# Seven-product pairs of a gated FFN: the next pair's first product ahead of this pair's last, a third buffer, low parts moved between two engines

## The chip, the cores and the metric

The kernel runs on one core of a Trainium2 chip (trn2). The metric is the device time of one execution in microseconds (us); lower is better. Five engines work side by side, each through its own queue and in order: TensorE (PE, matmuls; PEld is its weight load), VectorE (DVE), ScalarE (ACT), GpSimd (POOL) and SyncE (SP), which here issues the transfers. Engines wait for each other through counting semaphores.

## The reference, cut to what matters

Two layers of a decoder run over 512 prompt tokens and 64 new tokens (TOK = 576 columns), with model width 1024. A layer is FFN, token mixer, FFN, so that four FFNs take part:

```python
def ffn_half(h, g_pre, g_post, w_in, w_out):
    a = rmsnorm(h, g_pre) @ w_in
    gate, up = jnp.split(a, 2, axis=-1)
    return h + FFN_RESID * rmsnorm((jax.nn.silu(gate) * up) @ w_out, g_post)
```

`w_in` is 1024 x 5632 and `w_out` 2816 x 1024, all float32. The diff touches only how `rmsnorm(h) @ w_in` and the gate after it are computed and scheduled.

## The kernel before, in words

**Precision.** A float32 operand is split into a high part (ACT copies it to the fp32r type, `x_hi`, `w_hi`) and a low part (the rest, a subtraction, `x_lo`, `w_lo`). A product is three fp32r matmuls: high x high, high x low, low x high.

**Stages.** Six stages follow each other: ffn, mla, ffn, ffn, gla, ffn. In an FFN the input product has two phases. The first, "classic" phase takes 8 blocks of weights (128 x 1024, one block is one gate or up tile) straight: slots `raw[i]`, `w_hi[i]`, `w_lo[i]`, four of each. ACT makes the high part (line 754), POOL the low part (line 1233).

**The pairs.** The second phase takes the other 36 blocks as 18 pairs (`GRP` = 18), a gate block and an up block each. A pair's 2 x 2 block product is done in seven half-size products instead of eight (a Strassen-Winograd form): the weight blocks a11, a12, a21, a22 (128 x 512) give the sums s1 = a21 + a22, s2 = s1 + a11, s3 = a11 + a21, s4 = s2 + a12 (DVE, line 1563), and the activations give b11, b21, b22 and four sums t_0 to t_3 (each 128 x 4 x 288). PE computes in this order; `f_p` counts the products:

| product | weights x activations | PSUM bank | waits for |
|---|---|---|---|
| P1 | a11 x b11 | A, fresh | low part of a11 (POOL) |
| P2 | s1 x t_0 | C, fresh | low part of s1 (DVE) |
| P3 | s2 x t_3 | A, added | low part of s2, copy of P1 made |
| P4 | s4 x b22 | C, added | low part of s4, copy of P2 made |
| P5 | s3 x t_1 | A, added | low part of s3, copy of P3's state made |
| P6 | a12 x b21 | B, fresh | low part of a12 (POOL) |
| P7 | a22 x t_2, plain float32 | A, added | DVE has read A after P5 |

P1 to P6 are 12 matmuls each at line 2313, 128 x 288; P7 is 8 instructions at line 2353. Banks A, B, C alternate between two sets from pair to pair.

**DVE in pair g** (`group`, line 1643 on): last half of pair g-1 (line 1615, reads bank A after P7 of g-1), low part of s4 (line 1590), low part of the gated result of g-1 (line 1495), low part of s3, then s1 of pair g+1, P4's bank plus a copy (line 1597), scaling (1602), s2 of g+1, bank A after P5 (1636), product of the two (1640), low part of s1 of g+1, s4 of g+1, P6's bank plus the copy (1597), scaling (1602), s3 of g+1, low part of the gated result (1495 and 1497), low part of s2 of g+1. **ACT in pair g**: silu of g-1 (line 900), high part of s3 (873), high part of the gated result of g-1 (904, waits for DVE's line 1615), copy of P1's bank (896), copies after P2 and P3, high parts of a11 and s1 of g+1, silu, high parts of s2, s4, a12 of g+1. **POOL** does the low parts of a11 and a12 (line 1250). **SP** loads the four parts of pair g+1 (line 627): a22 into one of two buffers, the other three after all four sums of pair g stand.

**Ahead of the pairs.** DVE rebuilds x from its halves (`whole`, four times 128 x 1152, line 1540) and forms t_0 to t_3 (lines 1551, 1556) between the classic blocks, with POOL making the low parts of blocks 4 to 7 meanwhile.

Of the kernel before, what the change touches and what calls it, by code (L numbers as in the profile page):

```python
# [7 lines left out]
F32 = mybir.dt.float32  # L8
# [64 lines left out]
def hybrid_step(nc, io, stages=STAGES):  # L73
    pre_gain = PRE_GAIN
    with ExitStack() as ctx:
# [67 lines left out]
        t_f = [sb(f"t_f{i}", [P, HK, HALF], offset=h_at + i * T_W) for i in range(4)]  # L143
        t_lo = {i: sb(f"t_lo{i}", [P, HK, HALF], F32R, offset=h_at + i * T_W) for i in (0, 1, 3)}
# [183 lines left out]
        def forms(st):  # L328
# [13 lines left out]
            return made[r]  # L342

# [240 lines left out]
        def _(sp):  # L584
# [25 lines left out]
            def ffn(st):  # L610
# [15 lines left out]
                def part(dst, row_of, c, landed, g, i):  # L626
                    sp.dma_start(dst[:, :], w_in[f, FB + 2 * g + row_of + 4 * i, :, c * HK * P:(c + 1) * HK * P]).then_inc(landed, 16)

                def four(g, i):

                    a = g0 + g
                    if g >= 2:
                        sp.wait_ge(f_p, 7 * (a - 1) + 14 * i)
                    part(w[f"a22_{g % 2}"], 1, 1, f_a2[g % 2], g, i)
                    sp.wait_ge(f_sum, 4 * (a - 1) + 3 + 8 * i)
                    sp.wait_ge(f_alo, 2 * a + 4 * i)
                    part(w["a12"], 0, 1, f_a12, g, i)
                    sp.wait_ge(f_sum, 4 * a + 8 * i)
                    part(w["a21"], 1, 0, f_a2[g % 2], g, i)
                    part(w["a11"], 0, 0, f_a11, g, i)  # L640
# [109 lines left out]
        def _(act):  # L750
# [94 lines left out]
            def ffn(st):  # L845
# [56 lines left out]
                def high_part(g, c, n, half, i):
                    act.wait_ge(f_gu, n + 4 * i)
                    act.activation(gu[:, CLASSIC + g + 2 * i, half * HALF:(half + 1) * HALF], c[:, :], ACT.Copy).then_inc(s_guhi, 1)

                def last_half(g, i):
                    gate(c_1[g % 2], 5 * (g0 + g) + 5, i)

                def group(g, i, more):
# [1982 lines left out]
```

## Time and profile before

| | us |
|---|---|
| median of 3 runs | 2428.88 (2423.8 to 2429.35) |
| the profiled execution's own time | 2426.47 |
| its span on the core | 2424.8 |

| engine | busy us | share of the span |
|---|---|---|
| PE | 2308.0 | 95% |
| PEld | 2039.3 | 84% |
| DVE | 1336.3 | 55% |
| ACT | 967.8 | 40% |
| POOL | 685.5 | 28% |

The page says that a busy PE is not a PE at its peak, since matmuls overlap in the pipeline; so the start times of consecutive matmuls are what tells a wait. A row of the timeline gives the start in us from the span's start, the duration in us, engine, line, operation, tiles and shapes, and in square brackets the idle time of that engine just before it with what ended it.

### The profile page before, as it was taken

To read this page: it belongs to the slowest core of one execution; us is meant where nothing else is said; L and a number is where in the kernel's file an instruction comes from. 1 tells how busy PE (TensorE), PEld (TensorE's weight loads), DVE (VectorE), ACT (ScalarE), POOL (GpSimd) and SP (SyncE) were. 2 spreads that over 40 slices of the span, in tenths; PEclk is the share of its full clock that TensorE was granted. 3 is DMA by queue.
4 is the path that set the end of the run, shared out by engine and by line. 5 is a ranking of instruction groups with operands and counts; after the bars stand their busy time and mean duration, and the time that the engine had idled before them with its cause. 6 is when DMAs were issued, how large, how long until landed. Compare 5 with 4: busy or idle time off the path is not lost.

```text
span 2424.8 us, 37992 instructions
## 1 busy us (share of the span) xinstructions
PE 2308.0 (95%) x14176; PEld 2039.3 (84%) x14176; DVE 1336.3 (55%) x2545; ACT 967.8 (40%) x2014; POOL 685.5 (28%) x441
## 2 busy tenths in 40 slices
PE   8899999999899999999999999999999999999998
PEld 7888988986456889998888898888999789899887
DVE  5888700586421588881058888104566647788401
ACT  5445412614221645552254455225322444455322
POOL 2222243240312322224332222432344222222332
PEclk9999999999998999999999999999999999999999
DMA  3222332232671322224232222422211332222422
GB/s 124 74 88 83 97 122 87 70 111 82 196 233 53 109 79 87 83 75 144 87 109 79 87 88 71 145 86 82 70 53 56 152 99 98 75 87 84 143 85 84
DMA packets 100292, 237.53 MB, mean 98 GB/s; under 512 B 12268, under 2 KB 29165, under 8 KB 99854
## 3 DMA queue, kind: packets, MB, share of 16 engines
q1 hardware_dynamic: 97038, 224.62, 28.7%
q0 software_dynamic: 3072, 10.49, 1.3%
q8 instruction: 114, 1.87, 0.3%
q14 instruction: 68, 0.56, 0.1%
HBM read 220.17 MB, written 14.89 MB: 97 GB/s over the span
## 4 chain that ended last, share of the span: by engine, by line
PE 70%; DVE 8%; issue 8%; ACT 4%; SPq 3%; POOL 2%; DMA 2%; DVEq 0%; ACTq 0%; POOLq 0%
PE psum L2313 24%; PE psum L2251 7%; PE psum L2252 7%; PE psum L2253 7%; PE psum L2353 5%; PE psum L2117 3%; PE psum L2119 3%; PE psum L2118 3%; POOL w_lo L1233 2%; PE psum L2245 2%; PE psum L2244 2%; DVE s_r L1563 1%; SPq L493 1%; PE psum L2675 1%; ACT c L896 1%
## 5 line engine op out<-in xcount | busy, mean ns | idle before, releaser
L1233 POOL TENSOR_TENSOR w_lo<-raw,w_hi 128x1024 fp32r<-128x1024 f32 (+1 forms) x173 | 416.8, 2416 | 813.6 <-ACT w_hi L754 813.2
L1250 POOL TENSOR_TENSOR a_lo_r<-a_r,a_hi_r 128x512 fp32r<-128x512 f32 x144 | 193.0, 1341 | 700.6 <-ACT a_hi_r L873 485.7
L754 ACT ACTIVATE w_hi<-raw 128x1024 fp32r<-128x1024 f32 (+1 forms) x179 | 187.2, 1048 | 478.8 <-DMA raw<-ffn_out 349.7
L1394 DVE TENSOR_TENSOR y<-psum,g_post 128x512 f32<-128x512 f32 x48 | 32.5, 689 | 548.8 <-ACT y L768 548.2
L2117 PE MATMUL psum<-x_hi,w_hi 128*128 128x256 f32 (+1 forms) x1008 | 304.7, 302 | 0.3
L2118 PE MATMUL psum<-x_lo,w_hi 128*128 128x256 f32 (+1 forms) x1008 | 299.7, 297 | 0.0
L2119 PE MATMUL psum<-x_hi,w_lo 128*128 128x256 f32 (+1 forms) x1008 | 299.7, 297 | 0.0
L2251 PE MATMUL psum<-w_hi,gu 128*128 128x512 f32 x704 | 275.8, 392 | 0.6
L2252 PE MATMUL psum<-w_hi,gu 128*128 128x512 f32 x704 | 274.0, 389 | 0.0
L2253 PE MATMUL psum<-w_lo,gu 128*128 128x512 f32 x704 | 274.0, 389 | 0.0
L2313 PE MATMUL psum<-t_lo,s_hi_r 128*128 128x288 f32 x864 | 254.5, 295 | 0.0
L2313 PE MATMUL psum<-t_hi,s_hi_r 128*128 128x288 f32 x576 | 175.1, 304 | 49.0 <-ACT c L896 41.4
L873 ACT ACTIVATE s_hi_r<-s_r 128x512 fp32r<-128x512 f32 x288 | 181.1, 629 | 74.9 <-DVE s_r L1563 74.9
L1590 DVE TENSOR_TENSOR s_lo_r<-s_r,s_hi_r 128x512 fp32r<-128x512 f32 x288 | 199.4, 694 | 0.0
L2117 PEld LDWEIGHTS psum<-x_hi,w_hi 128*128 128x128 f32 x1008 | 192.9, 191 | 4.3 <-issue 1.8
L2118 PEld LDWEIGHTS psum<-x_lo,w_hi 128*128 128x128 f32 x1008 | 193.1, 192 | 0.2
L2119 PEld LDWEIGHTS psum<-x_hi,w_lo 128*128 128x128 f32 x1008 | 192.8, 191 | 0.0
L2313 PE MATMUL psum<-x_hi,a_hi_r 128*128 128x288 f32 x576 | 184.9, 321 | 3.5 <-DVE work L1483 3.5
L2313 PE MATMUL psum<-x_hi,s_lo_r 128*128 128x288 f32 x576 | 170.3, 296 | 0.0
L2313 PE MATMUL psum<-x_hi,s_hi_r 128*128 128x288 f32 x576 | 170.1, 295 | 0.0
L2313 PE MATMUL psum<-x_lo,a_hi_r 128*128 128x288 f32 x576 | 169.7, 295 | 0.0
L2313 PE MATMUL psum<-x_hi,a_lo_r 128*128 128x288 f32 x576 | 169.6, 294 | 0.0
(318 smaller groups left out, 5101.8 us busy)
## 6 DMA issues: line engine op xcount, KB each, us to landing
a_r<-ffn_in SPq DMA_DIRECT2D x288, 256.0 KB, 3.2
raw<-ffn_out SPq DMA_DIRECT2D x88, 512.0 KB, 3.5
raw<-ffn_in SPq DMA_DIRECT2D x32, 512.0 KB, 3.6
raw<-gla_in SPq DMA_DIRECT2D x25, 512.0 KB, 3.5
cache<-cache POOLq DMA_DIRECT2D x64, 160.0 KB, 4.9
cache<-cache SPq DMA_DIRECT2D x64, 160.0 KB, 5.1
c_k<-cache_kt SPq DMA_DIRECT2D x64, 128.0 KB, 3.1
keep<-h SPq DMA_DIRECT2D x12, 512.0 KB, 6.3
```

The lines of the kernel that those rows point to most:

```text
L754: act.activation(w_hi[slot][:, 0:w], raw[slot][:, 0:w], ACT.Copy).then_inc(s_hi, 1)
L873: act.activation(dst[:, :], src[:, :], ACT.Copy).then_inc(f_hi, 1)
L1233: pool.tensor_tensor(w_lo[slot][:, 0:w], raw[slot][:, 0:w], w_hi[slot][:, 0:w].bitcast(F32), ALU.subtract).then_inc(s_lo, 1)
L1250: pool.tensor_tensor(w[f"{name}_lo"][:, :], w[name][:, :], w[f"{name}_hi"][:, :].bitcast(F32), ALU.subtract).then_inc(f_alo, 1)
L1590: dve.tensor_tensor(w[f"{name}_lo"][:, :], w[name][:, :], w[f"{name}_hi"][:, :].bitcast(F32), ALU.subtract).then_inc(f_lo, 1)
L2117: pe.matmul(out, wh, xh, start=start, stop=False)
L2118: pe.matmul(out, wh, xl, start=False, stop=False)
L2119: return pe.matmul(out, wl, xh, start=False, stop=stop)
L2251: pe.matmul(dst, w[0], m[0], start=start, stop=False)
L2252: pe.matmul(dst, w[1], m[0], start=False, stop=False)
L2253: return pe.matmul(dst, w[0], m[1], start=False, stop=stop)
L2313: last = pe.matmul(out[:, 0:HALF], y, m[:, k, :], start=fresh and first, stop=end, skip_group_check=not fresh)
```

## The change

**PE.** P1 of pair g+1 is issued between P6 and P7 of pair g (`first`). Its bank condition is the single eviction or the last half of pair g-1.

**Buffers.** a22 has three buffers, by g mod 3: the two of before, and columns 288 to 415 of the first four k-rows of `x_lo`, which no product of the pairs reads. Rows there are 512 bytes with a stride of 2304 bytes. SP then loads a21 as soon as s3 of the pair before stands, a22 once P7 of three pairs back is done, a11 after POOL's low part of the last a11, and a12 after s4 and a12's low part.

**DVE and ACT order.** In pair g DVE now does: last half of g-1, low of s3, low of the gated result of g-1, s1 and s2 of g+1, P4's bank, scaling, bank A after P5, s3 and s4 of g+1, the product, P6's bank, scaling, low of s1, low of the gated result, low of s2, low of s4 (all g+1). ACT does: high of g-1's result, high of a11, copy after P2, high of s1, copy after P3, high of s2, silu, high of s3, high of s4, high of the result, silu of the second half, high of a12, copy of P1 of g+1. POOL keeps the low parts of a11 and a12.

**Ahead of the pairs.** The four `whole` go to the end of the stage before (`pre_factors`), into tiles `x_f` in space of `gu` not yet used; the low parts of classic blocks 4 to 7 go from POOL to DVE (`w_low`). All counts on semaphores follow.

```diff
+        x_f = [sb(f"x_f{i}", [P, HK, HALF], offset=g_at + (CLASSIC + i) * 2 * W4) for i in range(4)]
+        a22_x = sb("a22_x", [P, HK, TOK], offset=x_at + DT * W4)
...
+        def a_22(st, g):
+
+            if g % 3 == 2:
+                return a22_x[:, :, HALF:HALF + P]
+            return forms(st)[f"a22_{g % 3}"][:, :].rearrange("p (k c) -> p k c", k=HK)
... SP
+                for g in range(1, GRP):
+                    a = g0 + g
+                    sp.wait_ge(f_sum, 4 * (a - 1) + 3)
+                    part(w["a21"][:, :], 1, 0, f_a2[g % 2], g)
+                    if g == 2:
+                        sp.wait_ge(f_x, 8 * (f + 1))
+                    if g >= 3:
+                        sp.wait_ge(f_p, 7 * (a - 2) + 1)
+                    part(a_22(st, g), 1, 1, f_a2[g % 2], g)
+                    sp.wait_ge(f_alo, 2 * (a - 1) + 1)
+                    part(w["a11"][:, :], 0, 0, f_a11, g)
+                    sp.wait_ge(f_sum, 4 * a)
+                    sp.wait_ge(f_alo, 2 * a)
+                    part(w["a12"][:, :], 0, 1, f_a12, g)
... ACT
+                def copy_first(g):
                     a = g0 + g
+                    act.wait_ge(s_gulo, c0 + (2 * a if g == 0 else 2 * (a - 1)))
+                    copy_out(c_1[g % 2], ring(st, g, 0), first_product(g, a))
+
+                def group(g):
+                    a, more = g0 + g, g < GRP - 1
                     if g > 0:
...
+                        high_part(g - 1, c_1[(g - 1) % 2], 2 * a, 0)
                     if g == 0:
                         act.wait_ge(s_unit, u0 + 4 * CLASSIC)
-                        x_form(1, 6)
+                        x_form(1, 7)
+                    if more:
+                        hi_a11(a + 1)
...
+                    copy_out(c_3, ring(st, g, 1), 7 * a + 2)
+                    if more:
+                        hi_sum("s1", a + 1, 1, 2)
...
+                    copy_out(c_2, ring(st, g, 0), 7 * a + 3)
                     if more:
...
+                        hi_sum("s2", a + 1, 2, 3)
...
+                    gate(c_2, 5 * a + 2)
                     if more:
...
+                        hi_sum("s3", a + 1, 3, 5)
+                        hi_sum("s4", a + 1, 4, 4)
+                    high_part(g, c_2, 2 * a + 1, 1)
+                    gate(c_1[g % 2], 5 * a + 5)
                     if more:
...
+                        hi_a12(a + 1)
+                        copy_first(g + 1)
... POOL
             def ffn(st):
-                n = first_block[st] + SLOTS
-                pool.wait_ge(s_lo, n)
-                for j in range(FB - SLOTS):
-                    low(n + j)
...
+                for a in range(g0, g0 + GRP):
+                    part_low("a11", a, 1, 1)
+                    part_low("a12", a, 6, 6)
+                pool.wait_ge(s_lo, first_block[st] + FB)
... DVE
             def pre_factors(b):
 
+                if stages[b] == "ffn":
+                    for i in (0, 1, 3):
+                        whole(b, i)
                 dve.wait_ge(s_hroot, 2 * b + 2)
...
+                w_low(b0 + 4)
                 for hf in range(2):
                     gate_low(q0 + hf, hf, 0)
+                w_low(b0 + 5)
...
+                def group(g):
+                    a, more = g0 + g, g < GRP - 1
                     if g > 0:
...
+                        last_half(g - 1)
+                    low_form("s3", g, 4, 3)
                     if g > 0:
...
+                        low_part(g - 1, c_1[(g - 1) % 2], 2 * a, 0)
+                    if more:
+                        sum_1(g + 1)
                     if g == 0:
                         x_low_form(1, 3)
                     if more:
...
+                        sum_2(g + 1)
+                    plus(c_2, ring(st, g, 1), 3 * a + 3, 7 * a + 4)
+                    scaled(c_2, 1, 5 * a + 1)
...
+                    if more:
+                        sum_3(g + 1)
+                        sum_4(g + 1)
...
+                    plus(c_1[g % 2], ring(st, g, 2), 3 * a + 1, 7 * a + 6)
+                    scaled(c_1[g % 2], 0, 5 * a + 4)
                     if more:
...
+                        low_form("s1", g + 1, 2, 2)
+                    low_part(g, c_2, 2 * a + 1, 1)
                     if more:
...
+                        low_form("s2", g + 1, 3, 4)
+                        low_form("s4", g + 1, 5, 4)
... PE
+                def first(g):
+                    a = g0 + g
+                    pe.wait_ge(f_alo, 2 * a + 1)
+                    if g < 2:
+                        pe.wait_ge(s_evicted, u0 + 4 * CLASSIC - RING + 3 * g + 1)
+                    else:
+                        pe.wait_ge(f_gu, 2 * (a - 1))
+                    product(ring(st, g, 0), "a11", b_11, True)
...
                     product(b_b, "a12", b_21, True)
...
+                    if g < GRP - 1:
+                        first(g + 1)
+                    pe.wait_ge(f_c, 5 * a + 3)
```

## Rows read from the trace of the kernel before

**Rows 1.** Windows, one per FFN's pairs: length, busy us of each engine, clock, DMA.

```profile
73.73:299.20 225.47, 211.02 (x1441) 199.57 (x1441) 181.45 (x326) 112.13 (x236) 49.27 (x36) 1.00 0.27 87
875.23:1099.40 224.17, 211.03 (x1441) 199.58 (x1441) 180.02 (x326) 111.93 (x236) 49.72 (x36) 1.00 0.28 88
1298.88:1523.20 224.32, 211.08 (x1441) 199.63 (x1441) 180.09 (x326) 111.95 (x236) 49.71 (x36) 1.00 0.28 88
2050.40:2278.20 227.80, 213.63 (x1441) 201.66 (x1441) 180.38 (x326) 112.09 (x236) 49.24 (x36) 0.99 0.27 86
```

**Rows 2.** Timeline of PE in one settled pair: first matmul of each product.

```profile
939.79 0.51 PE L2313 MATMUL psum<-x_hi,a_hi_r 128*128 128x288 f32 x1
...
941.59 0.30 PE L2313 MATMUL psum<-t_hi,s_hi_r 128*128 128x288 f32 x1
...
943.88 0.37 PE L2313 MATMUL psum<-t_hi,s_hi_r 128*128 128x288 f32 x1 [0.54 <-ACT c L896]
...
945.55 0.29 PE L2313 MATMUL psum<-x_hi,s_hi_r 128*128 128x288 f32 x1
...
950.32 2.10 PE L2353 MATMUL psum<-t_f,a_r 128*128 128x288 f32 x8
952.05 0.51 PE L2313 MATMUL psum<-x_hi,a_hi_r 128*128 128x288 f32 x1
```

**Rows 3.** Timeline of DVE in the same pair.

```profile
940.37 1.49 DVE L1495 TENSOR_TENSOR gu<-c,gu 128x224 fp32r<-128x224 f32 x1
...
941.91 0.68 DVE L1590 TENSOR_TENSOR s_lo_r<-s_r,s_hi_r 128x512 fp32r<-128x512 f32 x1
942.51 0.44 DVE L1615 SCALAR_TENSOR_TENSOR c<-psum,c 128x288 f32<-128x288 f32 x1
942.88 0.68 DVE L1590 TENSOR_TENSOR s_lo_r<-s_r,s_hi_r 128x512 fp32r<-128x512 f32 x1
...
947.42 0.46 DVE L1597 TENSOR_TENSOR c<-psum,c 128x288 f32<-128x288 f32 x1 [1.37 <-PE psum L2313]
947.91 0.51 DVE L1602 TENSOR_TENSOR c<-c,r_pre 128x288 f32<-128x288 f32 x1
```

**Rows 4.** Timeline of DVE at the last pair's end: line 1495 alone.

```profile
1099.06 0.38 DVE L1495 TENSOR_TENSOR gu<-c,gu 128x224 fp32r<-128x224 f32 x1
```

**Rows 5.** Timelines of ACT and POOL in the same settled pair.

```profile
942.99 0.45 ACT L904 ACTIVATE gu<-c 128x288 fp32r<-128x288 f32 x1 [1.88 <-DVE c L1615]
943.34 0.69 ACT L896 ACTIVATE c<-psum 128x288 f32<-128x288 f32 x2
...
946.12 0.62 ACT L873 ACTIVATE a_hi_r<-a_r 128x512 fp32r<-128x512 f32 x1
...
940.25 1.36 POOL L1250 TENSOR_TENSOR a_lo_r<-a_r,a_hi_r 128x512 fp32r<-128x512 f32 x1 [4.31 <-PE psum L2353]
946.82 1.29 POOL L1250 TENSOR_TENSOR a_lo_r<-a_r,a_hi_r 128x512 fp32r<-128x512 f32 x1 [5.21 <-ACT a_hi_r L873]
```

**Rows 6.** Timelines of the first pair (second FFN): PE, DVE, SP, ACT.

```profile
875.23 0.40 PE L2313 MATMUL psum<-x_hi,a_hi_r 128*128 128x288 f32 x1 [0.87 <-DVE work L1483]
...
877.71 0.69 DVE L1563 TENSOR_TENSOR s_r<-s_r,a_r 128x512 f32<-128x512 f32 x1
...
881.42 1.28 SPq L627 DMA_DIRECT2D a_r<-ffn_in  x3
...
886.02 0.63 ACT L873 ACTIVATE a_hi_r<-a_r 128x512 fp32r<-128x512 f32 x1 [3.14 <-DMA a_r<-ffn_in]
```

**Rows 7.** Timelines ahead of the pairs (second FFN): DVE, and PE at block 7.

```profile
833.64 0.18 DVE L1432 RECIPROCAL h_r<-h_r 128x4 f32<-128x4 f32 x1 [3.51 <-ACT h_r L804]
...
863.16 1.35 DVE L1551 TENSOR_TENSOR t_f<-t_f,t_f 128x1152 f32<-128x1152 f32 x1
...
867.80 0.28 PE L2117 MATMUL psum<-x_hi,w_hi 128*128 128x256 f32 x1
```

**Rows 8.** Timeline of PE, first pair of the last FFN: P7.

```profile
2065.93 0.85 PE L2353 MATMUL psum<-t_f,a_r 128*128 128x288 f32 x1 [3.60 <-DVE c L1636]
```

More of the change, by code:

```diff
@@ L624, in ffn, with part @@
                 w, g0 = forms(st), GRP * f
[L626 to L640, printed above, removed]
+                def part(dst, row_of, c, landed, g):
+                    src = w_in[f, FB + 2 * g + row_of, :, c * HK * P:(c + 1) * HK * P]
+                    sp.dma_start(dst, src.rearrange("p (k c) -> p k c", k=HK) if len(dst.shape) == 3 else src).then_inc(landed, 16)
@@ L642, in ffn @@
                 classic_out(sp, st, 0)
                 wait_keep(sp, st)
-                part(w["a21"], 1, 0, f_a2[0], 0, 0)
-                part(w["a22_0"], 1, 1, f_a2[0], 0, 0)
-                part(w["a11"], 0, 0, f_a11, 0, 0)
+                part(w["a21"][:, :], 1, 0, f_a2[0], 0)
+                part(a_22(st, 0), 1, 1, f_a2[0], 0)
+                part(w["a11"][:, :], 0, 0, f_a11, 0)
                 classic_out(sp, st, 2)
-                part(w["a12"], 0, 1, f_a12, 0, 0)
+                part(w["a12"][:, :], 0, 1, f_a12, 0)
@@ L900, in gate, with high_part @@
                     act.activation(c[:, :], c[:, :], ACT.Silu).then_inc(s_silu, 1)
[L902 to L909, printed above, removed]
+                def high_part(g, c, n, half):
+                    act.wait_ge(f_gu, n)
+                    act.activation(gu[:, CLASSIC + g, half * HALF:(half + 1) * HALF], c[:, :], ACT.Copy).then_inc(s_guhi, 1)
@@ L1587, in low_form, with sum_3, sum_4 @@
+                def sum_3(g):
+                    add("s3", w["a11"], w["a21"], g0 + g, 5)
+                def sum_4(g):
+                    a = g0 + g
+                    dve.wait_ge(f_sum, 4 * a + 2)
+                    dve.wait_ge(f_a12, 16 * (a + 1))
+                    add("s4", w["s2"], w["a12"], a, 4)
+                def low_form(name, g, hi, summed):
                     a = g0 + g
-                    dve.wait_ge(f_hi, 6 * a + hi + 12 * i)
-                    dve.wait_ge(f_sum, 4 * a + summed + 8 * i)
+                    dve.wait_ge(f_hi, 6 * a + hi)
+                    dve.wait_ge(f_sum, 4 * a + summed)
@@ L2358, in ffn @@
                 pair(3)
-                group(0, 0)
-                group(1, 0)
-                for i in range((GRP - 2) // 2):
-                    group(2, i)
-                    group(3, i)
+                first(0)
+                for g in range(GRP):
+                    group(g)
                 pe.wait_ge(s_gulo, 2 * FT * f + 2 * CLASSIC)
```

273 lines of the change are left out of this document (106 added, 167 removed).

## The prediction

> **What bounds the kernel now.** I read the table of busy shares first: PE is busy 95% of the span, DVE 55%, so DVE's average hides nothing by itself. Then the windows, one for each FFN's 18 pairs [rows 1]: they are 225.47, 224.17, 224.32 and 227.80 us long, 901.76 us in all, 37% of the span, and PE is idle 13.1 to 14.5 us in each. Then PE's timeline of one settled pair [rows 2]. It lasts 952.05 - 939.79 = 12.26 us. Six products of 12 matmuls take 1.59 us each where nothing waits (950.32 - 945.55 = 4.77 for P4 to P6), P7 takes 1.73, and the product behind P7 takes 1.80. So a pair without a wait would take 1.80 + 5 x 1.59 + 1.73 = 11.48 us. The missing 0.78 us is one hole: P2 starts at 941.59, P3 at 943.88, 0.70 more than 1.59 (the row's idle 0.54 starts from the modelled end), and P3 itself, restarted, takes 0.08 more (943.88 to 945.55). It is ended by ACT's copy of P1's bank.
>
> Why is that copy late? Backwards [rows 3, 5]: the copy starts at 943.34, behind ACT's line 904 (942.99), which waits for DVE's line 1615 (942.51), which is queued behind line 1590 (941.91) and line 1495 (940.37). That last one took 1.49 us, where the same instruction alone takes 0.38 [rows 4]: 1.11 us more, and POOL's low part of a11 runs from 940.25 to 941.61 beside it. An instruction of DVE with two SBUF inputs that comes 0.12 us after POOL's waits until POOL is through.
>
> The Trainium skill ("SBUF — State Buffer", Who interferes with whom) says that the second of two such instructions blocks for the whole of the first; here 1.11 us of POOL's 1.29 to 1.36 are lost, and the measurement decides.
>
> **The change part by part.**
>
> *P1 ahead of P7.* Its copy now has P7 and P2 (1.73 + 1.80 us) before P3 wants it, instead of P2 alone. The 0.78 us hole goes, if nothing takes its place. Three things could be late next; I walk one pair with the start of P2 as 0, so P3 starts at 1.80, P4 3.39, P5 4.98, P6 6.57, P1 of the next pair 8.16, P7 9.75, P2 again 11.48. A product's bank can be read 1.87 us after its start (P4 at 945.55, DVE's line 1597 at 947.42) [rows 2, 3]. Steps on DVE: 0.60 for a 512-wide instruction (941.91 to 942.51), 0.37 for a 288-wide one (942.51 to 942.88), 0.49 from the addition to the scaling that needs it; lines 1495 and 1497 together 941.91 - 940.37 - 1.11 = 0.43 [rows 3, 4]. ACT: 0.35 from line 904 to the next, 0.52 for a 512-wide high part (0.62 less the 0.10 overlap seen at 942.99), 0.48 from DVE's line 1615 to ACT's 904, 0.54 from a copy's start to PE's product [rows 2, 3, 5].
>
> DVE is free until P5's bank can be read: 4.98 + 1.87 = 6.85. From there its queue is full: bank A 0.37, s3 0.60, s4 0.60, product 0.37, addition 0.49, scaling 0.37, low of s1 0.60, low of the result 0.43, low of s2 0.60, then POOL's low part of a12, whose high part ACT finishes in just this stretch, 1.11, then low of s4 0.60. That is 6.14, up to 12.99. The last half follows and frees ACT 0.48 later (13.47), ACT writes the high part of the result (0.35), the high part of a11 (0.52), and the copy after P2, which lets P4 of the next pair start 0.54 later: 14.88. P4 is due at 11.48 + 3.39 = 14.87. So a second loop, P4 to P4 over DVE, POOL and ACT, takes 1.59 + 1.87 + 6.14 + 0.48 + 0.35 + 0.52 + 0.54 = 11.49 us, against PE's own 11.48. The two are equal; since any scatter of one then adds, I take 11.55.
>
> *Without that cover* the other waits have room. The low part of s1 starts at 9.65 and is there at 10.4 for P2 at 11.48; that of s2 at 11.4, or 12.5 behind the lock, for P3 at 13.28; the copy after P3 lets P5 go at about 4.7, due at 4.98. The transfers: SP is released by s3 (starts at 7.22, stands at 7.9) instead of by all four sums; the third of three loads is used 3.75 us after its issue (882.27, when the first starts at 881.42, to 886.02) [rows 6], so a11 is there at 7.9 + 0.9 + 3.75 = 12.6, 1.2 us before ACT wants it at 13.8. The strided third buffer (512-byte pieces, which this row does not show) may take some tenths more or nothing: bounds 0 and 1 us, both inside the 1.2.
>
> *The first pair.* P1 of pair 0 no longer waits for both evictions (idle 0.87 [rows 6]), but P3 does not profit. DVE begins s3 at 877.71 as before, s4 stands at 879.05, ACT's high parts of s4 and a12 take 2 x 0.52, the copy starts at 880.1, P3 at 880.6. Then ACT's order puts the high part of a11 ahead of the copy after P2, and a11 lands only at 878.5 + 0.85 + 3.75 = 883.1; P4 starts at 883.1 + 0.52 + 0.54 = 884.2 where 882.2 was due: a new stall of 1.9 us, between 0 (load in time) and 3. P2 of pair 1 then starts 4 x 1.59 + 1.73 later, at 892.2, which is 17.0 us after the window's start.
>
> *Ahead of the pairs.* The first three `whole` at 1.27 us each (1.35 less overlap, a like 128 x 1152 instruction at 863.16) fill DVE's idle 3.51 us ahead of the reciprocals [rows 7]: 0.3 us too long, with ACT and PE still on other work, so 0. The low parts of four classic blocks go to DVE at about 1.2 us each. The tightest is block 7: DVE is at 863.16, two sums of 1.27 and the low part 1.2 make 866.9, PE wants it at 867.80 [rows 7]. So 0, from -0.2 to 1 us per FFN if that cover goes. POOL's idle time costs nothing. Its locks on DVE vanish there, which frees nothing on PE.
>
> **The sum.** An FFN's window is 17.0 (to P2 of pair 1) + 16 T + 9.9 (pair 17: 1.80 + 4 x 1.59 + 1.73). With T = 11.55 it is 211.7, four of them 846.8, against 901.8: 55 us less. On the profiled execution's own time, 2426.5, this gives 2371.5; the median of the runs is 2.4 us higher, so 2374.
>
> **The rivals.** 0.1 us in T is 6.4 us.
>
> *A, better:* the DVE loop does not bind and a11 lands in time: T 11.48 and the front's 1.9 us gone, 4.5 + 7.6 less: 2362. For it: the loops are equal only to 0.01. Against it: ACT's order.
>
> *B, half way:* POOL's low part of a11 gets in ahead of s1 in part of the pairs. In the walk the order of the two is close: after line 1615 DVE starts s1 1.35 us later (0.48 + 0.45 + 0.05 for ACT's result, 0.37 for its low part), POOL arrives 0.48 + 0.35 + 0.62 + 0.08 = 1.53 later (0.08 as from 946.74 to 946.82 [rows 5]). If DVE loses, s1 is 1.1 us later, its high part too, and the copy after P3 behind it, so P5 stalls. The loop is then 1.87 + 6.14 + 0.48 + 0.35 + 0.70 + 1.11 + 0.73 + 0.52 + 0.54 = 12.44. In the six pairs of each FFN with the strided buffer (s1 waits for it): 4 x 6 x 0.9 = 21 us: 2396.
>
> *C, no change:* the same in all pairs: T = 12.44, 17 + 199 + 9.9 = 226, 904 in all: 2431. The 0.18 us margin speaks against it.
>
> *D, slower:* as C, and each of POOL's two locks costs its whole 1.29 instead of 1.11 (the arrival falls at the start of a DVE instruction, and both loops carry both): T = 12.8, 4 x (26.9 + 204.8) = 926.8: 2454. It is slower by over 0.3% from T = 12.5 on. Against it: row 940.37.
>
> *E:* on the forecast's loop the lock costs the whole of POOL's 1.36 instead of 1.11: T = 11.74 and 2386. Row 940.37 speaks against it too.
>
> The Trainium skill ("SBUF — State Buffer", Who interferes with whom) states the rule behind E, the second waits for the whole of the first; this case's row shows 1.11 us.
>
> *F:* the two stalls of the first pair let the clock drop, as in the last FFN, where after 3.60 idle the first instruction of P7 took 0.85 [rows 8] and P7 4.2 instead of 2.1 us. 3 us per FFN, 12 in all: 2386.
>
> *G, it does not do what it says:* P1 of the next pair finds its bank taken. It needs the last half of pair g-1, done at about 2.0, and is due at 8.16. I give this nothing.
>
> **How the numbers follow.** Forecast 0.60, A 0.10, B 0.12, C 0.05, D 0.06, E and F together 0.07. The forecast's own spread is T from 11.48 to 11.7, 2369 to 2384. The range reaches over A, E, F and to B: 2360 to 2397. It leaves out C, D and a part of B. 0.3% is 7 us, about what a measurement of this kernel can tell: faster 0.89 (forecast, A, B, E, F), within 0.3% 0.05 (C), slower 0.06 (D).
>
> **What would show each step.** PE's timeline: line 2313 on a11 directly ahead of line 2353, pairs 11.5 to 11.6 apart, no idle time ahead of P3. Windows of 210 to 213 us. Ahead of P4 at most 0.1 us idle, ended by ACT's line for the copy. DVE: a low part (line 1590's successor) of about 1.8 us once per pair, the one of s4. First pair: about 2 us ahead of P4, with ACT waiting for a11's transfer. Wrong would be: idle time ahead of P5 (B, C), a11's landing later than 5 us in settled pairs, or PE waiting at block 7 for a low part.

## The result, and the profile after

| | before | after |
|---|---|---|
| median of the runs, us | 2427.38 (4 runs) | 2366.01 (4 runs, 2361.64 to 2368.19) |
| profiled execution's own time, us | 2426.47 | 2368.19 |
| its span, us | 2424.8 | 2366.5 |
| PE busy, share of the span | 95% | 97% |

The ratio is 0.9747, 95% interval 0.9726 to 0.9767: 61 us or 2.5% faster; 2374 was forecast, 55 less than the 2428.88 known then. It was measured again beside the experiments: 2363.41 (5 runs), ratio 0.9743 (0.9727 to 0.9759).

The windows of the four FFNs' pairs in the changed kernel, as in [rows 1] (window, its length, busy us of PE, PEld, DVE, ACT and POOL, clock, DMA share, GB/s):

```profile
72.77:283.80 211.03, 208.37 (x1442) 199.64 (x1441) 190.71 (x321) 110.08 (x233) 60.75 (x36) 1.00 0.29 93
861.05:1072.72 211.67, 208.49 (x1442) 199.62 (x1441) 190.66 (x321) 110.11 (x233) 60.05 (x36) 1.00 0.29 93
1271.27:1482.43 211.16, 208.38 (x1442) 199.63 (x1441) 190.83 (x322) 110.14 (x233) 60.67 (x36) 1.00 0.30 93
2008.78:2219.85 211.07, 208.36 (x1442) 199.62 (x1441) 190.69 (x322) 110.11 (x233) 60.69 (x36) 1.00 0.30 93
```

Together they are 844.9 us, against 901.8 before: 56.8 of the 58.3 us that the profiled executions differ by. PE is now idle 2.7 to 3.2 us in a window instead of 13.1 to 14.5. From the second pair on, the time from P2 to P2 is 11.58 us in the mean instead of 12.33, over 64 pairs 48 us less. The first pairs give 6 us, nearly all of it in the last FFN (14.5 us instead of 20.2), where P7 had waited 3.60 us before [rows 8] and the granted clock was 0.66 from 2062.30 to 2070.20. DVE and POOL are each busy some 10 us more per window: they block each other more than before, in places where it mostly costs nothing.

One settled pair (one that follows another pair of its FFN) of the second FFN. PE: P7 of the pair before, then P2, P4 and P7 of this one, as [rows 2]:

```profile
933.47 2.10 PE L2362 MATMUL psum<-t_f,a_x 128*128 128x288 f32 x8
935.20 0.51 PE L2313 MATMUL psum<-t_hi,s_hi_r 128*128 128x288 f32 x1
938.61 0.37 PE L2313 MATMUL psum<-x_hi,s_hi_r 128*128 128x288 f32 x1
945.04 2.10 PE L2362 MATMUL psum<-t_f,a_r 128*128 128x288 f32 x8
```

P7 to P7 is 945.04 - 933.47 = 11.57 us, against 12.26. The starts of all seven products, read off the same timeline with P2 as 0, are P3 1.81, P4 3.41, P5 5.09, P6 6.68, P1 of the next pair 8.26, P7 9.84. The hole ahead of P3 is gone; the one product that is too long is P4, 1.68 us instead of 1.59. Of the 64 pairs that follow another settled pair, 63 lie within 0.03 of 11.57. The other one takes 11.93: there a11 lands late and P4 waits 0.20 us for the copy behind it.

```profile
1053.58 0.63 ACT L883 ACTIVATE a_hi_r<-a_r 128x512 fp32r<-128x512 f32 x1 [0.24 <-DMA a_r<-ffn_in]
```

(P7's operand `a_x` is the third buffer; P7 itself shows no difference.)

DVE in that pair, as [rows 3]:

```profile
934.43 2.37 DVE L1596 TENSOR_TENSOR s_lo_r<-s_r,s_hi_r 128x512 fp32r<-128x512 f32 x2
936.72 0.45 DVE L1621 SCALAR_TENSOR_TENSOR c<-psum,c 128x288 f32<-128x288 f32 x1
...
938.06 0.68 DVE L1569 TENSOR_TENSOR s_r<-a_r,a_r 128x512 f32<-128x512 f32 x1
938.91 1.53 DVE L1569 TENSOR_TENSOR s_r<-s_r,a_r 128x512 f32<-128x512 f32 x1 [0.16 <-PE psum L2313]
...
942.16 0.46 DVE L1641 SCALAR_TENSOR_TENSOR c<-psum,c 128x288 f32<-128x288 f32 x1 [0.65 <-PE psum L2313]
...
946.00 2.38 DVE L1596 TENSOR_TENSOR s_lo_r<-s_r,s_hi_r 128x512 fp32r<-128x512 f32 x2
948.30 0.44 DVE L1621 SCALAR_TENSOR_TENSOR c<-psum,c 128x288 f32<-128x288 f32 x1
```

ACT and POOL, as [rows 5]:

```profile
937.20 0.45 ACT L914 ACTIVATE gu<-c 128x288 fp32r<-128x288 f32 x1 [2.44 <-DVE c L1621]
937.55 0.62 ACT L883 ACTIVATE a_hi_r<-a_r 128x512 fp32r<-128x512 f32 x1
938.08 0.39 ACT L906 ACTIVATE c<-psum 128x288 f32<-128x288 f32 x1
```

```profile
934.54 1.71 POOL L1253 TENSOR_TENSOR a_lo_r<-a_r,a_hi_r 128x512 fp32r<-128x512 f32 x1 [6.22 <-ACT a_hi_r L883]
938.25 1.64 POOL L1253 TENSOR_TENSOR a_lo_r<-a_r,a_hi_r 128x512 fp32r<-128x512 f32 x1 [2.00 <-ACT a_hi_r L883]
```

This is the forecast's second loop, from P4 to P4 over DVE, POOL and ACT. From bank A's reading to the last half DVE's queue is never empty: 948.30 - 942.16 = 6.14 us, with POOL's 1.71 us beside the low part of s4 (two such instructions take 2.38 instead of 1.29). Then ACT: 0.48 to line 914, 0.88 to the copy, 0.53 to P4.

The first pair (second FFN), as [rows 6]: PE, then DVE's sums and ACT.

```profile
865.73 0.37 PE L2313 MATMUL psum<-t_hi,s_hi_r 128*128 128x288 f32 x1 [1.35 <-DVE s_lo_r L1596]
869.20 0.37 PE L2313 MATMUL psum<-x_hi,s_hi_r 128*128 128x288 f32 x1 [1.64 <-ACT c L906]
```

```profile
862.81 0.69 DVE L1569 TENSOR_TENSOR s_r<-a_r,a_r 128x512 f32<-128x512 f32 x1
```

```profile
868.13 0.63 ACT L883 ACTIVATE a_hi_r<-a_r 128x512 fp32r<-128x512 f32 x1 [1.44 <-DMA a_r<-ffn_in]
868.66 0.39 ACT L906 ACTIVATE c<-psum 128x288 f32<-128x288 f32 x1
```

P4 waits 1.64 us for a copy that stands behind a11's landing: the stall that was forecast, at 1.9.

### The profile page after: what moved, and what is told of

Read it like the earlier page. It is cut to its first block, busy times and chain, and to the rows that moved or that the text cites. A ratio compares the mean times of both kernels' runs of the same rounds, so it can differ in the third digit from the quotient of the medians.

```text
span 2366.5 us, 38028 instructions
## 1 busy us (share of the span) xinstructions
PE 2297.0 (97%) x14176; PEld 2039.4 (86%) x14176; DVE 1372.5 (58%) x2561; ACT 964.2 (41%) x2014; POOL 688.8 (29%) x425
## 3 DMA queue, kind: packets, MB, share of 16 engines
q8 instruction: 114, 1.87, 0.3%
## 4 chain that ended last, share of the span: by engine, by line
PE 85%; DVE 5%; SPq 3%; ACT 3%; DMA 2%; issue 2%; POOL 0%; DVEq 0%; ACTq 0%; POOLq 0%
PE psum L2313 28%; PE psum L2251 7%; PE psum L2252 7%; PE psum L2253 7%; PE psum L2117 6%; PE psum L2362 6%; PE psum L2119 6%; PE psum L2118 6%; PE psum L2244 2%; PE psum L2245 2%; SPq L501 1%; PE psum L2682 1%; DMA a_r<-ffn_in 1%; ACT y L778 1%; SPq L552 1%
## 5 line engine op out<-in xcount | busy, mean ns | idle before, releaser
L1240 POOL TENSOR_TENSOR w_lo<-raw,w_hi 128x1024 fp32r<-128x1024 f32 (+1 forms) x157 | 373.6, 2386 | 743.4 <-ACT w_hi L764 743.2
L1253 POOL TENSOR_TENSOR a_lo_r<-a_r,a_hi_r 128x512 fp32r<-128x512 f32 x144 | 239.7, 1665 | 708.8 <-ACT a_hi_r L883 708.8
L1596 DVE TENSOR_TENSOR s_lo_r<-s_r,s_hi_r 128x512 fp32r<-128x512 f32 x288 | 268.9, 955 | 0.8
L2313 PE MATMUL psum<-t_hi,s_hi_r 128*128 128x288 f32 x576 | 185.0, 321 | 5.4 <-DVE s_lo_r L1596 5.4
L2313 PE MATMUL psum<-x_hi,s_hi_r 128*128 128x288 f32 x576 | 175.4, 304 | 5.9 <-ACT c L906 5.9
L2313 PE MATMUL psum<-x_hi,a_hi_r 128*128 128x288 f32 x576 | 169.4, 294 | 0.0
```

What stands on the lines that cost most here:

```text
L1240: pool.tensor_tensor(w_lo[slot][:, 0:w], raw[slot][:, 0:w], w_hi[slot][:, 0:w].bitcast(F32), ALU.subtract).then_inc(s_lo, 1)
L1253: pool.tensor_tensor(w[f"{name}_lo"][:, :], w[name][:, :], w[f"{name}_hi"][:, :].bitcast(F32), ALU.subtract).then_inc(f_alo, 1)
L1596: dve.tensor_tensor(w[f"{name}_lo"][:, :], w[name][:, :], w[f"{name}_hi"][:, :].bitcast(F32), ALU.subtract).then_inc(f_lo, 1)
L2313: last = pe.matmul(out[:, 0:HALF], y, m[:, k, :], start=fresh and first, stop=end, skip_group_check=not fresh)
```

## Experiments

Each kernel was run beside the kernel before, on the same chip; ratios are to that kernel. T is the median time from P2 to P2 of the settled pairs, "first pair" the same time for pair 0 (the median of the four FFNs, or the spread), both in us in the profiled execution.

| kernel | median us (runs) | ratio (95%) | T | first pair |
|---|---|---|---|---|
| after, again | 2363.41 (5) | 0.9743 (0.9727 to 0.9759) | 11.57 | 14.5 |
| P1 behind P7 | 2363.7 (4) | 0.9747 (0.9728 to 0.9766) | 11.59 | 14.9 |
| swap alone | 2462.3 (4) | 1.0148 (1.0123 to 1.0172) | 12.8 | 14.5 to 17.5 |
| copy order alone | 2405.99 (4) | 0.9896 (0.9862 to 0.993) | 12.02 | 15.5 to 20.2 |
| copy ahead of a11 | 2353.6 (5) | 0.9707 (0.969 to 0.9725) | 11.49 | 13.4 |
| no low a12 | 2362.37 (4) | 0.9725 (0.9696 to 0.9755) | 11.53 | 14.6 |
| low s4 behind last half | 2385.16 (4) | 0.9813 (0.9777 to 0.9849) | 11.94 | 14.5 |
| low parts back | 2364.65 (4) | 0.9742 (0.971 to 0.9773) | 11.57 | 15.3 (one 17.4) |
| two a22 buffers | 2492.96 (6) | 1.0266 (1.0237 to 1.0295) | 13.4 | 14.5 |
| copy ahead of a11, again | 2354.68 (5) | 0.9701 (0.9679 to 0.9723) | 11.49 | 13.5 |
| + first copy early | 2352.97 (5) | 0.9694 (0.9668 to 0.972) | 11.49 | 13.5 |
| + both copies early | 2352.01 (5) | 0.9683 (0.9659 to 0.9707) | 11.49 | 13.2 (one 13.9) |

### P1 behind P7, in the changed kernel

```
                     product(b_b, "a12", b_21, True)
-                    if g < GRP - 1:
-                        first(g + 1)
...
                     last.then_inc(f_p, 1)
+                    if g < GRP - 1:
+                        first(g + 1)
```

> The changed kernel with one thing undone: PE issues P1 of the next pair behind P7 again, as before the change (counts on f_p follow). Theory Q (the queues did it): P1 starts 9.75 us into the pair, its bank can be read at 11.7, ACT has been free since 10.8 and copies at once, so P3, due at 13.3, never waits; the loop P4 to P4 over DVE, POOL and ACT is untouched. T stays 11.57, the time is 2366, within 3. Theory S (the step of the prediction: the swap itself removes the hole, since the copy needs P7 and P2 as cover): the 0.7 us ahead of P3 comes back, T about 12.25, 2366 + 64 x 0.68 = 2410.

Measured: 2363.7, single pairs 11.56 to 11.61, P3 1.59 us after P2 with no wait. Undoing the swap costs nothing that the times can tell. The hole is not closed by the place of P1.

### The swap alone, in the kernel before

```
+                    if g < GRP - 1:
+                        first(g + 1)
...
-                    product(b_a, "a11", b_11, True)
```

> The kernel before with the PE swap alone: P1 of the next pair ahead of P7, all queues of DVE, ACT, SP and POOL in their old order. Theory Q: the copy of P1 stands behind line 904 and line 1615 in their queues wherever P1 is; P7 is done before line 1615's turn in either order. T stays 12.26 and the hole stays ahead of P3: 2427, within 4. Theory S: T falls to about 11.5, 2427 - 64 x 0.7 = 2382 or less.

Measured: 2462.3, 36 us slower than before, which neither theory gave. The hole ahead of P3 grew. PE's group of P2 and P3 (line 2313), first in the kernel before, then in this one, and the wait in one pair of this one; columns of the groups: busy us, mean ns, idle before with its releasers.

```profile
L2313 PE MATMUL psum<-t_hi,s_hi_r 128*128 128x288 f32 x576 | 175.1, 304 | 49.0 <-ACT c L896 41.4 <-DVE s_lo_r L1590 7.6
```

```profile
L2313 PE MATMUL psum<-t_hi,s_hi_r 128*128 128x288 f32 x576 | 191.2, 332 | 81.4 <-ACT c L896 73.8 <-DVE s_lo_r L1590 7.6
```

```profile
996.91 0.38 PE L2313 MATMUL psum<-t_hi,s_hi_r 128*128 128x288 f32 x1 [1.32 <-ACT c L896]
```

```profile
995.55 0.45 DVE L1615 SCALAR_TENSOR_TENSOR c<-psum,c 128x288 f32<-128x288 f32 x1
...
999.48 0.69 DVE L1563 TENSOR_TENSOR s_r<-a_r,a_r 128x512 f32<-128x512 f32 x1 [1.92 <-DMA a_r<-ffn_in]
1000.45 0.46 DVE L1597 TENSOR_TENSOR c<-psum,c 128x288 f32<-128x288 f32 x1 [0.28 <-PE psum L2313]
1000.95 1.47 DVE L1602 TENSOR_TENSOR c<-c,r_pre 128x288 f32<-128x288 f32 x1
```

The wait on the copy, which stands behind line 1615, is 73.8 of the 81.4 us, against 41.4 of 49.0 before. P7, now a product later, frees a22's buffer later, and SP's loads for the pair stand behind that: DVE's s1 waits for its data until 2.57 us after P3 (999.48 - 996.91), in the kernel before until 1.47 after it (P3 at 943.88 [rows 2]):

```profile
945.35 0.69 DVE L1563 TENSOR_TENSOR s_r<-a_r,a_r 128x512 f32<-128x512 f32 x1 [0.82 <-DMA a_r<-ffn_in]
```

ACT's high part of a11 and POOL's low part come late with it, and POOL's lock, which fell into DVE's idle time, now falls on the scaling: 1.47 us where it took 0.51 [rows 3]. So P3 to P3 carries a second lock: 13.1 us in that pair. A part of the 36 us is the clock: in six places PE's matmuls start 0.24 us apart instead of 0.13 (83 of them, an estimate of 9 us), for example behind a wait of 2.07 us ahead of P3, with a granted clock of 0.58 from 906.70 to 910.50. The chain is read from the trace and not shown by a run of its own; the next experiment shows a lock that falls into the same stretch of DVE's queue, and the one with two buffers shows what it costs when the other loads stand behind a22's.

### The copy's place in ACT's queue alone, in the kernel before

```
-                    if g > 0:
-                        high_part(g - 1, c_1[(g - 1) % 2], 2 * a, 0, i)
...
                     copy_out(c_1[g % 2], ring(st, g, 0), a, 1, i)
+                    if g > 0:
+                        high_part(g - 1, c_1[(g - 1) % 2], 2 * a, 0, i)
```

> The kernel before with one edit: ACT takes the copy of P1's bank ahead of the high part of the gated result of the pair before (line 904) instead of behind it. PE's order, DVE's order, SP's order and the buffers are those of before. Theory Q (ACT's order made the hole; the place of P1 on PE is worth nothing): the copy runs when P1 is done, P3 starts 1.80 us after P2, T falls from 12.26 to 11.5 to 11.6, 68 pairs by 0.7 us is 48 less: 2380, between 2375 and 2390. Rival (the copy was only the last of several equal waits; low s2 on DVE or the copy after P2 takes its place at once): T stays above 12, 2410 or more.

Measured: 2405.99, 21 us less. PE's two groups that changed:

```profile
L2313 PE MATMUL psum<-t_hi,s_hi_r 128*128 128x288 f32 x576 | 176.1, 306 | 8.4 <-DVE s_lo_r L1590 8.0
L2353 PE MATMUL psum<-t_f,a_r 128*128 128x288 f32 x576 | 163.1, 428 | 13.1 <-DVE c L1636 12.1
```

Of the 41.4 us that P3 waited for ACT at most 0.4 are left; two moved lines did that. But T fell only from 12.25 (the same median in the kernel before) to 12.02, a third of the 0.7 us that I expected: DVE's queue, with both of POOL's locks in it, is late next. The first pairs also got longer (15.5 to 20.2 us, before 14.2 to 20.2), mostly by PE's wait for line 1636 ahead of P7, which is 12.1 us in all against 6.0 before.

```profile
978.69 0.46 DVE L1602 TENSOR_TENSOR c<-c,r_pre 128x288 f32<-128x288 f32 x1
979.07 1.78 DVE L1563 TENSOR_TENSOR s_r<-s_r,a_r 128x512 f32<-128x512 f32 x1
980.77 0.44 DVE L1636 SCALAR_TENSOR_TENSOR c<-psum,c 128x288 f32<-128x288 f32 x1
```

The lock falls on s2, directly ahead of the reading of bank A that P7 needs (P7 at 981.27). That is where the rival was right. What takes it away is the changed kernel's order on DVE, with s1 and s2 at the head of the pair and s3 and s4 behind bank A: there the same s2 takes 1.53 us (938.91) and the readings of P4's and P5's banks still come in time. How much of that is DVE's order and how much the earlier loads (here s1 still waits for its data until 977.60) no run shows apart.

### The copy after P2 ahead of the high part of a11

```
-                    if more:
-                        hi_a11(a + 1)
                     if a >= 1:
                         act.wait_ge(f_gu, 2 * a - 1)
                     copy_out(c_3, ring(st, g, 1), 7 * a + 2)
                     if more:
+                        hi_a11(a + 1)
```

> The changed kernel with two steps of ACT's queue swapped: the copy after P2 ahead of the high part of a11. Loop theory: the loop over DVE, POOL and ACT that ends at P4 loses 0.52 us and no longer binds, T falls from 11.57 to PE's own 11.48 (17 x 4 x 0.09 = 6 us), and the first pair's wait for a11's landing ahead of P4 (1.5 to 1.8 us in the trace) goes, 4 x 1.6 = 6: 12 us less than the changed kernel, about 2354. Rival: the 0.09 us is PE's own (the matmuls ahead of P5 are slower for another reason): 6 us less, about 2360. Second rival: POOL's low part of a11, now 0.35 later, falls on s2, and P5 or P6 waits: no gain or a loss.

Measured: 2353.6, and 2354.68 when it was measured again. P7 to P7 in the latter:

```profile
935.83 2.10 PE L2361 MATMUL psum<-t_f,a_r 128*128 128x288 f32 x8
947.32 2.10 PE L2361 MATMUL psum<-t_f,a_r 128*128 128x288 f32 x8
```

11.49 us, PE's own time, and the first pair is 1.1 us shorter. So the second loop did bind, as walked, with one term missing (below).

### GpSimd without its reading of a12

```
+                    if name == "a12":
+                        pool.memset(w["a12_lo"][:, :].bitcast(F32), 0.0).then_inc(f_alo, 1)
+                        return
```

> The changed kernel without GpSimd's low part of a12: GpSimd writes zeros in its place, so it reads nothing from SBUF while DVE does the low part of s4 (the low part of a12 is left out of the products). Loop theory (P4 waits for ACT's copy, ACT for DVE's queue, which carries GpSimd's 1.1 us): that low part of s4 takes 0.7 instead of 1.77 us, P4 waits for nothing, T falls from 11.57 to 11.48, 68 x 0.09 = 6 us less: 2358; the first pair keeps its 1.5 us. Rival (the 0.08 us at P4 is PE's own, nothing of the loop): T stays 11.57, 2364. Second rival: zeros written by GpSimd block DVE just as its reading does: low part of s4 still 1.7 us, 2364.

Measured: 2362.37, single pairs 11.49 to 11.55. DVE, then POOL:

```profile
954.83 1.29 DVE L1599 TENSOR_TENSOR s_lo_r<-s_r,s_hi_r 128x512 fp32r<-128x512 f32 x2
956.09 0.46 DVE L1624 SCALAR_TENSOR_TENSOR c<-psum,c 128x288 f32<-128x288 f32 x1
...
957.68 1.79 DVE L1572 TENSOR_TENSOR s_r<-a_r,a_r 128x512 f32<-128x512 f32 x1 [0.16 <-PE psum L2316]
```

```profile
954.93 0.52 POOL L1254 MEMSET a_lo_r<- 128x512 f32 x1 [7.55 <-ACT a_hi_r L883]
957.62 1.29 POOL L1256 TENSOR_TENSOR a_lo_r<-a_r,a_hi_r 128x512 fp32r<-128x512 f32 x1 [2.17 <-PE psum L2316]
```

A GpSimd instruction that only writes leaves DVE alone (1.29 for two, not 2.38). The Trainium skill ("SBUF — State Buffer", Who interferes with whom) says the same, that a DVE instruction with two SBUF inputs contends with one that reads SBUF and "not with one that only writes it"; the trace agrees. The last half comes 1.1 us earlier, and with it a11's low part on POOL, which now gets in 0.06 us ahead of s1 (1.79 us). P4 now waits for nothing and takes 1.59 us, but the copy after P3, behind s1's high part, ends just when P5 is due: no idle time shows, P5's first matmul takes 0.34 us instead of 0.29, and P5 up to 1.65 us. So half the forecast 6 us came (windows 841.5 instead of 844.5), and rival B's way to P5 took the rest.

### The low part of s4 behind the last half

```
                         last_half(g - 1)
+                        low_form("s4", g, 5, 4)
...
                         low_form("s2", g + 1, 3, 4)
-                        low_form("s4", g + 1, 5, 4)
```

> The changed kernel with one edit: DVE does the low part of s4 behind the last half instead of ahead of it. The last half, ACT's high part of the result, its high part of a11 and with it GpSimd's low part of a11 then come up to 1.7 us earlier, so GpSimd's low part of a11 can start ahead of DVE's s1, and s1, its high part and the copy after P3 come late. Theory of rival B and C of the prediction (second loop over s1): P5 waits 0.3 to 0.9 us, T 11.9 to 12.4, plus 22 to 56 us: 2386 to 2420. Rival (only the copy after P2 matters, which now comes earlier): T 11.48, 2358.

Measured: 2385.16, T 11.94 in 52 of the 64 settled pairs and 11.49 in 10. PE, P5:

```profile
969.84 0.38 PE L2313 MATMUL psum<-x_hi,s_hi_r 128*128 128x288 f32 x1 [0.21 <-ACT c L906]
```

POOL's low part of a11 started at 966.48, just ahead of DVE's low part of the result (966.59), which took 1.55 us, and s1 stands behind that. P5 is 0.38 us late, P5 itself 0.09 longer. Rival B's mechanism is real; in the changed kernel the low part of s4 ahead of the last half keeps it away. A pair mostly has the whole stall or none; two of the 64 lie between (11.83 and 11.75).

### Low parts of blocks 4 to 7 back on GpSimd

```
-                w_low(b0 + 6)
...
+                n = first_block[st] + SLOTS
+                pool.wait_ge(s_lo, n)
+                for j in range(FB - SLOTS):
+                    low(n + j)
```

> The changed kernel with the low parts of classic blocks 4 to 7 back on GpSimd, as before; the four whole instructions stay early. It tests the part ahead of the pairs. If the low parts on DVE brought P3 of the first pair forward (it starts 1.4 us earlier than I forecast), each FFN's first pair gets later again: 0.5 to 1.4 us per FFN, 2 to 6 us in all: 2366 to 2370. If they brought nothing: 2364, within 0.1%. If GpSimd's longer instructions there lock DVE, more than 6 us.

Measured: 2364.65, no difference that can be told. But in the profiled execution P3 of the first pair comes 3.83 us after P2 instead of 3.10, and in three FFNs the first pair is 0.7 to 0.9 us longer. In the third FFN it is 17.4 us, 2.9 longer: PE idles 2.08 us ahead of P3 and 1.16 ahead of P4, and the granted clock falls to 0.50, the lower of its two levels (1.2 instead of 2.4 GHz). The window (the clock is the third figure from the end):

```profile
1272.40:1276.00 3.60, 3.51 (x15) 3.54 (x16) 1.88 (x2) 1.40 (x3) 1.14 (x1) 0.50 0.03 7
```

DVE and POOL ahead of the pairs:

```profile
843.24 3.57 DVE L1563 SCALAR_TENSOR_TENSOR t_f<-t_f,x_f 128x1152 f32<-128x1152 f32 x1
```

```profile
842.49 3.11 POOL L1240 TENSOR_TENSOR w_lo<-raw,w_hi 128x1024 fp32r<-128x1024 f32 x1 [14.06 <-ACT w_hi L764]
```

DVE's instruction takes 3.57 instead of 1.35 us beside POOL's low part.

### Two buffers for a22 instead of three

```
-            if g % 3 == 2:
-                return a22_x[:, :, HALF:HALF + P]
...
-                    if g == 2:
-                        sp.wait_ge(f_x, 8 * (f + 1))
-                    if g >= 3:
-                        sp.wait_ge(f_p, 7 * (a - 2) + 1)
+                    if g >= 2:
+                        sp.wait_ge(f_p, 7 * (a - 1) + 1)
```

> The changed kernel with two buffers for a22 (pair mod 2) instead of three: SP then waits for P7 of two pairs back ahead of a22's load, and the loads of a11 and a12 stand behind it. If the third buffer and its 512-byte pieces are worth nothing: within 0.1% of the changed kernel (2363 to 2366), T 11.57. If the later load of a22 holds a11's back past the moment ACT wants it (the walk left 1.2 us): T above 11.6, each 0.1 us is 7 us. In the odd case that the strided buffer cost something: T the same in all pairs, 0 to 2 us less.

Measured: 2492.96, some 129 us slower than the changed kernel and slower than the kernel before. The prediction had the third buffer's worth at nothing, and what I expected of this run named the way it works without a price. PE's group of P4 and P5, then SP's queue and ACT in one pair:

```profile
L2309 PE MATMUL psum<-x_hi,s_hi_r 128*128 128x288 f32 x576 | 181.3, 315 | 115.4 <-ACT c L902 115.4
```

```profile
990.23 0.33 SPq L638 DMA_DIRECT2D a_r<-ffn_in  x1
994.17 0.80 SPq L638 DMA_DIRECT2D a_r<-ffn_in  x2
```

```profile
997.65 0.63 ACT L879 ACTIVATE a_hi_r<-a_r 128x512 fp32r<-128x512 f32 x1 [1.44 <-DMA a_r<-ffn_in]
998.19 0.39 ACT L902 ACTIVATE c<-psum 128x288 f32<-128x288 f32 x1
```

a21 leaves when s3 stands (990.23). Then SP stands until the P7 that PE is about to do has used the buffer (994.17, 3.9 us later), and a11's load stands behind a22's. ACT's high part of a11 starts 5.61 us after P7's start (PE's P7 is at 992.04), in the changed kernel 4.08 (937.55 - 933.47), and the copy after P2 stands behind it: 13.1 us in this pair. The third buffer is not spare room; it takes P7 out of the chain that leads to a11. PE waits 115.4 us for that copy. Most of the rest is the clock again: in eight pairs 111 matmuls start 0.24 us apart instead of 0.13 (an estimate of 12 us), for example behind an idle time of 2.24 us ahead of P4, at a granted clock of 0.50:

```profile
930.30:933.30 3.00, 3.00 (x13) 3.00 (x14) 0.00 (x0) 1.17 (x3) 0.88 (x1) 0.50 0.00 0
```

### The first pair: copies ahead of the landing

```
                 pair(3)
+                copy_first(0)
...
-                copy_first(0)
                 for g in range(GRP):
```

> As e3, and at the front of the pairs ACT takes the copy of the first P1 ahead of the high parts of s3, s4 and a12. Theory M (in the first pair P5 waits for the copy after P3, which stands behind a11's landing in ACT's queue, and the landing is tied to SP's loads): P3 starts 0.7 us earlier, P5 waits 0.7 us longer, nothing gained: 2354, first pair 13.5 us. Rival (P3's wait sets the end of the first pair): 0.7 us per FFN, 3 us less: 2351.

Measured: 2352.97. P3 starts at 2.32 instead of 3.09 us, P5 at 6.98, and the windows are 835.2 us both with and without it: nothing gained. P5 waits for the copy after P3, behind a11's landing.

```
-                    if more:
+                    if g > 0 and more:
...
                     copy_out(c_2, ring(st, g, 0), 7 * a + 3)
+                    if g == 0:
+                        hi_a11(a + 1)
+                        hi_sum("s1", a + 1, 1, 2)
```

> As e8, and in pair 0 of each FFN the copy after P3 too goes ahead of the high part of a11 (and that of s1). Theory M: no copy of the first pair stands behind the landing any more; P3 at 2.4, P4 at 4.0, P5 at 5.6 us after P2, first pair 12.2 us instead of 13.5, 4 x 1.3 = 5 us less than e3: 2349. Rival (the landing comes back as a wait of pair 1's P2, since s1's high part waits behind it): no gain, 2354.

Measured: 2352.01; in three FFNs the first pair takes 13.2 us, not 12.2, and pair 1 11.59; in the other FFN 13.9. The copy was no longer the last wait:

```profile
864.77 0.37 PE L2315 MATMUL psum<-x_hi,s_hi_r 128*128 128x288 f32 x1 [0.60 <-DVE t_lo L1553]
```

P5 of the first pair also needs the low part of its own factor, which DVE does behind s1. 0.3 us of the 1.3 came in those three, the other FFN gave it back, and the windows are 835.2 as before. The last three versions can't be told apart; each beats the changed kernel by about 10 us (0.4%), and that gain is the first edit's.

## Why the prediction was right, and where it was not

**The hole ahead of P3: right in reading, wrong in its cause.** The prediction followed the copy back to line 904, line 1615 and POOL's lock, and then gave the cure to another edit, P1 ahead of P7: "Its copy now has P7 and P2 (1.73 + 1.80 us) before P3 wants it, instead of P2 alone." A longer time between P1 and P3 helps only if the copy can use it; in ACT's old queue it stood behind line 904 and could not. The swap alone made it 36 us slower, the copy's new place alone took the 41.4 us of waiting away, and with the new queues the swap is worth nothing. This is the step that failed: the swap as the cause. That the number came out all the same is luck in this step, since the diff held both edits. One reading in it was wrong too: the POOL instruction at 940.25, which the prediction calls the low part of a11, is that of a12. P1 of that pair, which needs the low part of a11, had already started at 939.79 [rows 2]; a11's is the one at 946.82, behind ACT's high part at 946.12 [rows 5]. The sum is not touched, since the walk of the new queues puts a12's lock on the low part of s4, where it was found. No run took the lock out of the kernel before, so the lock's share in the old hole is read from the trace.

**The second loop: right, one term short.** The walk gave DVE 6.14 us; it took 6.14. ACT's 0.48, 0.35 + 0.52 and 0.54 were 0.48, 0.88 and 0.53. What was missing is 0.09: a product that had to wait takes 1.68 us instead of 1.59, which [rows 2] showed for P3 and which I left out for P4. 1.68 + 1.87 + 6.14 + 0.48 + 0.88 + 0.53 = 11.58, measured 11.57, forecast 11.55 (11.49 and some for scatter). There was next to no scatter; that the allowance for it, 0.06, nearly made up for the missing 0.09 is luck. Rival A was this kernel with one exchange in ACT's queue: T 11.49 and the front half a stall shorter, 2354 where A said 2362.

**Rivals B and C: not here, but close.** The order of POOL's a11 and DVE's s1 came out as walked, DVE ahead by 0.19 us (938.06 and 938.25; forecast 0.18). Where it tips, with the low part of s4 moved, T is 11.94 and only P5 is late, by 0.38 and 0.09. That is no measure of the forecast's 12.44: with the low part of s4 out of the stretch ahead of the last half, DVE there waits 0.57 us for P7 (line 1621 at 964.94), so the loop of the forecast is open. No run has the tipped order in the changed kernel's own queues.

**E and the lock's size.** The low part of s4 takes 1.09 us longer (2.38 - 1.29) though POOL's instruction lasts 1.71: POOL waited itself for the first 0.4 (1.71 less its 1.29), and of the rest DVE loses most, not all. The row of before (1.11) decided this rightly, against E's 11.74 and D. G did not come either: P1 of the next pair starts on time, 1.58 us after P6.

**F, the clock: not here.** In the changed kernel PE idles 1.35 and 1.64 us in the first pair shown, and the granted clock is 1.00 in all four windows. The rival is real all the same: with the low parts back on POOL one FFN had it, and its first pair was 2 us longer than the other three (F said 3 us per FFN).

**The transfers: no wait in 63 of 64 settled pairs, as forecast, but the reason was not priced.** a11 lands 1.0 us after P2 in the median (forecast 1.1), 1.4 before ACT wants it. The one late pair is one whose a22 went to the third buffer. The view of that buffer's tile says

```profile
DMA to landing us min/median/max: 2.9/3.1/5.2
```

where plain a22 loads at the same place of the queue take 2.9 in the median and 4.6 at most: the strided pieces cost some 0.2 us, inside the forecast's bounds, and one late landing in 64 (none when the kernel was measured again). That the pieces made the 5.2 is not shown. What the prediction left out is what the buffer does: without it the release of SP by s3 is worth nothing, and the pair is 1.8 us longer.

**The first pair.** Its stall ahead of P4 was 1.5 to 1.8 us (forecast 1.9), by a11's landing, as forecast. But "P3 does not profit" and "its locks on DVE vanish there, which frees nothing on PE" were wrong. The first P1 now starts 0.14 us after the matmul ahead of it instead of 1.17, 1.03 earlier, since no eviction holds it; and the first of DVE's two sums here starts 1.76 us behind that P1 (862.81 - 861.05) instead of 2.48. (It is s3 now; the row at 877.71, which the prediction calls s3, is s4, since the kernel before made s4 first.) Against PE's classic products DVE is thus 1.75 us earlier, and P3 1.7. With the low parts back on POOL that sum starts 2.49 us behind P1, so 0.7 of the 1.75 is the missing lock; the other 1.0, which the early `whole` may explain, was not tried alone.

**The sum.** Forecast windows 846.8. T was 0.027 us longer in the mean (64 x 0.027 = 1.7 more), the first pair better: pair 1's P2 was forecast 17.0 us after the window's old start and came 14.52 + 1.58 - 1.03 = 15.07 after it in the mean, 4 x 1.93 = 7.7 less. That makes 840.8. The windows, measured 844.9, each begin 1.03 us earlier than those of before: 840.8 on the old starts. So the sum was 1.7 us too low in the pairs and 7.7 too high at the front, and a part of its closeness is that these cancel. Of these 6.0 us below the forecast 3.3 are seen in the profiled execution (2368.2 against 2371.5). The other 2.7 went elsewhere, 2.2 of them between the first FFN's pairs and the second's. That stretch takes 571.6 to 578.3 us in the profiled executions of the changed kernel and of two variants that do not touch it (P1 behind P7, copy ahead of a11), so it may be scatter alone.

## To carry to other kernels

When a wait is traced back through a queue, price the edit that changes the queue, not the one that gives more time in front of it; if the diff holds both, ask of each what it would do alone. A buffer that looks spare may be what keeps a late consumer out of an in-order DMA queue: before costing it at nothing, name what is queued behind the load that would wait. When a loop is summed from parts, take a product's time as it is after a wait, not as it is unhindered. Two neighbouring instructions of one kind (the low parts of a11 and a12 here) are told apart by what released them, before one of them is blamed.

## What the hardware showed that I had not expected

- In the changed kernel a POOL instruction that starts under a running 512-wide DVE instruction takes 1.64 to 1.71 us instead of 1.29, and DVE's next one is held: each pays, DVE 0.8 us (s2, 1.53) to 1.1, POOL 0.4.
- With wider instructions the lock is longer: POOL's 128 x 1024 beside DVE's 128 x 1152 made 3.57 us out of 1.35 (2.2 us more, against 0.8 to 1.1).
- A loop over PE, DVE, POOL and ACT repeats to the last digits: 63 of 64 pairs within 0.03 us of 11.57, and all 64 at 11.49 once it does not bind.
- Two stalls near each other may or may not cost clock: with 2.08 us idle and then 1.16 the granted clock stood at 0.50 for 3.6 us in one FFN, and it did not fall so in the other three, whose P3 waited as long (2.08 us) and whose P4 waited 1.4 to 1.5 us.
